# Moving a quarter of the modulation projection from a feed-forward stage into a delta-rule recurrence, with an idle product ahead of each solve

## The chip, the core and the metric

The kernel runs as one program on one core of a Trainium2 chip. The metric is device time in microseconds from start to end of the program. All data is float32.
## What is computed

Two blocks of two layers each work on 512 tokens of width 1024. The first block has attention mixers and gated feed-forward layers (1024 to 2816 to 1024). The second block has a mixer with a bidirectional gated delta rule and pooling, an expert-choice feed-forward, a short-convolution mixer and a second expert-choice feed-forward. Each norm of the second block is modulated by vectors that depend on the conditioning alone:

```python
for i in range(DEPTH):                                        # second block, DEPTH = 2
    sh1_l, sc1_l, g1_l, sh2_l, sc2_l, g2_l = jnp.split(jax.nn.silu(c) @ ada_w[i] + ada_b[i], 6, axis=-1)
    hl = modulate(rms_norm(xl, norm_mix[i]), sh1_l, sc1_l)    # then the mixer, scaled by g1_l
    ...
    hl2 = modulate(rms_norm(xl, norm_ffn[i]), sh2_l, sc2_l)
    xl = xl + g2_l[:, None] * expert_choice_ffn(hl2, router[i], w_gate[i], w_up[i], w_down[i])

# gated delta rule, chunks of 64 tokens, 4 heads, forwards and backwards; context (256 tokens) first, then the 512 tokens
t_mat = eye + where(strict, kk * decay, 0) * beta[..., None]
u = solve(t_mat, v * beta[..., None]);  wk = solve(t_mat, k * (beta * exp(gam))[..., None])
w = u_c - einsum(wk_c, s);  s = cd_c * s + einsum(kd_c, w)
```

`ada_w` is (2, 1024, 6144). Of layer 1, the last three of the six vectors (sh2, sc2, g2) are first read in the last quarter of the program, by the norm before the second expert layer and by that layer.

## The kernel before

**The modulation.** Class `Modulation` computes both layers' 6144 outputs in 12 groups of 1024 outputs, each group in 4 parts, 48 parts in all. A part reads one panel of 1 MB (`fetch`, two buffers in `arena`). The stationary operand is `cond`, two columns (the conditioning of the tokens and of the context), and the moving operand is weights, 256 columns. One group's outputs are laid over four strips of PSUM partitions (0, 32, 64, 96), so that the four products of a round stand in four column strips of the array. A part is 8 products (L1129): 2 of the 8 tiles of the contraction times 4 strips. After four parts `keep` copies 2 by 256 values from each strip, and after all twelve groups `turn` transposes everything (96 small transposes, L1146) and `add` adds it to the biases.

**Where it runs.** All of it runs in the first gated feed-forward of the first block. PE works there through 20 quads of seven blocks each (`GatedUnits.quad_products`, L467: 4 products per block, 8 records). `ada_between` puts one part after the second, fourth and sixth block of a quad: parts 2 to 47 stand in quads 0 to 15, and `turn` stands in quad 17. `mod.part` waits for its panel; SyncE issues the panels in a row with the feed-forward's own weights.

**The recurrence.** `even_mixer` runs `DeltaChain` in 6 steps (`STEPS`; steps 0 and 1 are the context, `LAT_FROM` = 2). A step handles 128 tokens in each of two directions d. The order of each engine is written out by hand:

- `keys` (L2167), `level_z` (L2180) and `level_update` (L2194) build the inverse of the triangular matrix in 6 levels (`LEVELS`), each product being 64 by 64. After each, VectorE masks or subtracts (`level_mask` L2439, `level_x` L2443, `level_y` L2447), and PE waits for that.
- `solve` (L2251, L2258) uses the finished inverse `Y`. It waits for `y_solved`, `k_done` and `v_done` of both directions, from step 2 on also for `qk_done`, which VectorE's `within_rows` (L2455) gives.
- In the next step `use_state` (L2274) waits until ScalarE has copied the result of the solve (`keep_solved`, L2368). Then `new_state` (L2284) and `outputs` (L2296, L2300) update the state.
- `turn_keys` (L2205) and `turn_values` (L2218) transpose keys and values.

`stay_busy(k, pe, bank, n, cols)` (L114) issues n products whose result nobody reads. The recurrence has one of 256 columns ahead of `use_state` in steps 1 to 5, and three after `turn_keys` in steps 1 and 2. SyncE loads the output projection's four panels (`out.fetch`, L3912) before step 2 into four buffers (three in `h`, one in `gate_rows`), and for each step from 2 on the gate rows (`fetch_gates`, L2133) and the growth rows (`fetch_growth`, L2144), in this order, each behind its own waits.

## Time and profile before

| | us |
|---|---|
| median of 3 runs | 2789.36 (2783.68 to 2789.53) |
| the profiled execution, its own time | 2787.13 |
| span of its trace | 2785.3 |
| first gated feed-forward with the modulation, 415 to 712 | 297 |
| recurrence, six steps, 1726 to 1941 | 215 |

A row of the timeline gives the start of a run of like records, the time they cover, the engine, the line, the tiles and shapes, the number of records, and in brackets how long the engine sat idle before and what it waited for. [...] The time around the span of the profiled execution is 1.8 us.

### The profile page before, as it was taken

What the parts mean: (1) busy time and instruction counts of PE and PEld (TensorE: products, weight loads), DVE (VectorE), ACT (ScalarE), POOL (GpSimd) and SP (SyncE); (2) the same over time, 40 slices, a digit from 0 to 9 for tenths busy, and PEclk for the clock granted to TensorE, in tenths of its full rate; (3) what the DMA queues carried; (4) which work ended last, traced back from release to release, by engine and by line L of the source; (5) the groups of instructions that cost most, each with busy time, mean ns of one, the idle gap of its engine ahead of it and who ended that gap; (6) DMA issues with size and microseconds to landing.
All of it is one profiled execution on the core that took longest, in us unless ns stands there. A gap on an engine that the chain in (4) does not pass through costs nothing. (4 is left out here: it accounts for less than half of the span.)

```text
span 2785.3 us, 36571 instructions
## 1 busy us (share of the span) xinstructions
PE 2710.5 (97%) x15316; PEld 1801.6 (65%) x15316; DVE 1162.6 (42%) x2250; ACT 525.9 (19%) x1164; POOL 626.2 (22%) x450
## 2 busy tenths in 40 slices
PE   8999999999999999999999999899989999998998
PEld 5564477777886445888888755888733338873333
DVE  2325534444413233544433485656232235652223
ACT  1344410000001133110000232433110120011011
POOL 3250004333341010344443410010010003531000
PEclk9999999999999999999999999999999999999999
DMA  8211026775222211222221402100399972239994
GB/s 268 103 46 46 31 91 248 266 266 183 84 98 88 91 72 46 91 84 83 72 83 42 190 17 78 39 21 7 154 367 421 420 301 76 92 123 365 421 421 198
DMA packets 70045, 431.23 MB, mean 155 GB/s; under 512 B 8203, under 2 KB 9018, under 8 KB 25721
## 3 DMA queue, kind: packets, MB, share of 16 engines
q1 hardware_dynamic: 65080, 412.56, 38.7%
q0 software_dynamic: 4800, 16.33, 1.7%
q8 instruction: 122, 2.00, 0.3%
q14 instruction: 43, 0.34, 0.0%
HBM read 422.41 MB, written 13.79 MB: 157 GB/s over the span
## 5 line engine op out<-in xcount | busy, mean ns | idle before, releaser
L467 PE MATMUL bank<-h,weight_ring 128*128 128x256 f32 x960 | 230.3, 383 | 1.1 <-DVE arena L391 1.0
L467 PEld LDWEIGHTS bank<-h,weight_ring 128*128 128x128 f32 x960 | 179.8, 190 | 38.4 <-issue 13.7
L622 PE MATMUL bank<-arena,weight_ring 128*128 128x256 f32 x704 | 155.0, 379 | 0.0
L467 PE MATMUL bank<-h,arena 128*128 128x256 f32 x640 | 151.2, 379 | 0.0
L622 PEld LDWEIGHTS bank<-arena,weight_ring 128*128 128x128 f32 x704 | 133.8, 190 | 18.4 <-issue 0.4
L3038 PE MATMUL bank<-weight_slots,tokens_T 128*64 128x512 f32 x592 | 141.7, 593 | 2.1 <-issue 2.1
L467 PEld LDWEIGHTS bank<-h,arena 128*128 128x128 f32 x640 | 121.7, 190 | 16.4
L427 POOL TENSOR_TENSOR arena<-weight_ring 128x512 f32<-128x512 f32 x40 | 52.8, 1320 | 352.5 <-PE bank L467 309.5
L3581 PE MATMUL bank<-h,weight_slots 128*128 128x256 f32 (+1 forms) x384 | 128.9, 491 | 0.8 <-ACT h L2705 0.8
L3077 PE MATMUL bank<-logits_or_select,h 128*128 128x512 f32 x256 | 118.2, 600 | 1.7 <-DVE h L3207 1.7
L622 PE MATMUL bank<-arena 128*128 128x256 f32 x528 | 117.1, 380 | 0.0
L325 PE MATMUL bank<-arena,weight_ring 128*128 128x256 f32 (+1 forms) x384 | 116.4, 454 | 0.0
L1440 PE MATMUL bank<-weight_ring,h 128*128 128x512 f32 x256 | 113.3, 597 | 0.0
L622 PEld LDWEIGHTS bank<-arena 128*128 128x128 f32 x528 | 100.3, 190 | 14.3 <-DVE x L664 0.4
L1440 PE MATMUL bank<-h,weight_ring 128*128 128x512 f32 (+2 forms) x304 | 107.4, 507 | 0.6 <-DVE h L273 0.6
L3581 PEld LDWEIGHTS bank<-h,weight_slots 128*128 128x128 f32 x384 | 71.5, 190 | 56.1 <-issue 46.5
L3038 PE MATMUL bank<-weight_ring,tokens_T 128*64 128x512 f32 x432 | 105.0, 592 | 0.0
L3038 PEld LDWEIGHTS bank<-weight_slots,tokens_T 128*64 128x64 f32 x592 | 49.6, 137 | 81.1 <-issue 79.2
L897 DVE COPY arena<-bank 128x512 f32<-128x512 f32 x96 | 61.9, 685 | 91.8 <-PE bank L906 62.5
L3198 DVE TENSOR_TENSOR hidden<-bank,hidden 128x512 f32<-128x512 f32 x16 | 11.1, 691 | 211.5 <-PE bank L3038 211.5
L325 PEld LDWEIGHTS bank<-arena,weight_ring 128*128 128x128 f32 x384 | 71.2, 190 | 39.0 <-issue 32.6
L1440 PEld LDWEIGHTS bank<-weight_ring,h 128*128 128x128 f32 x256 | 47.6, 190 | 62.9 <-issue 59.5
(607 smaller groups left out, 4746.0 us busy)
## 6 DMA issues: line engine op xcount, KB each, us to landing
arena<-in_ada_w SPq DMA_DIRECT2D x48, 1024.0 KB, 6.9
weight_ring<-in_gu SPq DMA_DIRECT2D x44, 1024.0 KB, 4.9
weight_slots<-in_w_up SPq DMA_DIRECT2D x42, 1024.0 KB, 26.0
weight_slots<-in_w_down SPq DMA_DIRECT2D x34, 1024.0 KB, 21.5
weight_slots<-in_w_gate SPq DMA_DIRECT2D x32, 1024.0 KB, 23.2
weight_ring<-in_w_gate SPq DMA_DIRECT2D x32, 1024.0 KB, 23.2
weight_ring<-in_w_down SPq DMA_DIRECT2D x30, 1024.0 KB, 24.1
weight_ring<-in_down SPq DMA_DIRECT2D x32, 704.0 KB, 4.4
```

Of the source, the lines that this page charges most:

```text
L325: m = pe.matmul(bank, self.slots[i].buf[:, at * P:(at + 1) * P], self.src(c)[:, lo:hi], start=(c == 0), stop=(c == self.kt - 1))
L427: g.tensor_tensor(s1, self.block(q, 1, 0), self.block(q, 1, 1), ALU.add).then_inc(self.summed.sem, 1)
L467: m = pe.matmul(self.bank(q, i), weights[:, c * P:(c + 1) * P], tokens[:, c, :], start=(c == 0), stop=(c == 3))
L622: m = pe.matmul(self.bank(u, name), lhs[:, j * P:(j + 1) * P], rhs, start=(j == 0), stop=(j == self.DEPTH - 1))
L897: v.tensor_copy(self.prob_T[:, c % 2, s, :], self.k.bank[:, 4 + s, :]).then_inc(self.copied.sem, 1)
L1440: m = pe.matmul(out, lhs, rhs, start=(c == 0), stop=(c == last - 1))
L3038: m = pe.matmul(self.k.bank[e * CAP:(e + 1) * CAP, 3 + j, :], self.tok_T[:, r % 2, 4 * half + c, e * CAP:(e + 1) * CAP], slot.buf[:, c * D ...
L3077: m = pe.matmul(self.k.bank[:, 2 if n % 2 == 0 else 5, :], self.y[:, self.place(r), c * P:(c + 1) * P], self.sel[:, self.place(r), :], sta ...
L3198: v.tensor_tensor(self.hid[:, :], self.k.bank[:, 4, :], self.hid[:, :], ALU.mult).then_inc(self.product.sem, 1)
L3581: m = pe.matmul(self.bank(n)[:, 0:hi - lo], slot.buf[:, at:at + P], self.h[:, c, lo:hi], start=(c == 0), stop=(c == KT - 1))
```

## The change

`Modulation` keeps 36 parts in 9 groups (layer 0, and the first half of layer 1). A new class `LateModulation` computes the other 12 parts, 3 groups, in the recurrence: one part ahead of `use_state` in steps 1 and 2 and two in steps 3 to 5; two parts after `turn_keys` in steps 1 and 2. The weights are laid out so that a late part covers all 8 tiles of the contraction and a quarter of the columns: 32 products of 64 columns each, in four strips. The idle products at these places go. `solve` now waits for keys, values and queries first, then issues one idle product of 256 columns, and then waits for `y_solved`. Four buffers hold the late panels, the same four that `out.fetch` fills later; each panel of either kind is issued when the part that read the buffer is done.

```diff
 class Modulation:
-    STRIPS, STRIP, WIDTH, GROUPS, PARTS = 4, 32, 256, 12, 4
+    STRIPS, STRIP, WIDTH, GROUPS, PARTS, LAYER = 4, 32, 256, 9, 4, 24
...
+class LateModulation:
+    FIRST, GROUPS, DEPTH = 9, 3, 4
...
+    def fetch(self, sp, n, weights):
+        if n >= self.DEPTH:
+            after(sp, self.done, n - self.DEPTH)
+        sp.dma_start(self.panels[self.place(n)], weights[n]).then_inc(self.landed[self.place(n)].sem, 16)
+
+    def part(self, pe, n):
+        g, i = divmod(n, Modulation.PARTS)
...
+        w = Modulation.WIDTH // Modulation.PARTS
+        for t in range(KT):
+            for s in range(Modulation.STRIPS):
+                at, panel = s * STRIP, (t * Modulation.STRIPS + s) * w
+                m = pe.matmul(self.bank(g)[at:at + 2, i * w:(i + 1) * w], self.cond[:, t, :], self.panels[self.place(n)][:, panel:panel + w],
+                              start=(t == 0), stop=(t == KT - 1))
+        m.then_inc(self.done.sem, 1)
+
+    def keep(self, v, g):
+        after(v, self.done, (g + 1) * Modulation.PARTS - 1)
+        v.tensor_copy(self.rows[:, g, :], self.bank(g)).then_inc(self.kept.sem, 1)
...
+    def turn(self, pe):
...
+        for g in range(self.GROUPS):
+            for j in range(2):
+                m = pe.matmul(out[:, g, :, j], self.rows[:, g, j * P:(j + 1) * P], self.k.ident[:, 0:P:STRIP], start=True, stop=True)
...
     def solve(self, pe, j):
         for d in range(2):
-            after(pe, self.y_solved[d], LEVELS * (j + 1) - 1)
             after(pe, self.k_done[d], j)
             after(pe, self.v_done[d], j)
             if j >= LAT_FROM:
                 after(pe, self.qk_done[d], j - LAT_FROM)
+        stay_busy(self.k, pe, 6, 1, HALF)
+        for d in range(2):
+            after(pe, self.y_solved[d], LEVELS * (j + 1) - 1)
...
+        PARTS_AT = {(1, 0): (0,), (1, 1): (1, 2), (2, 0): (3,), (2, 1): (4, 5), (3, 0): (6, 7), (4, 0): (8, 9), (5, 0): (10, 11)}
...
+                late.fetch(sp, 0, a["ada_late"])
...
-                for i in range(4):
-                    out.fetch(sp, i, a["ev2_out"])
+                late.fetch(sp, 1, a["ada_late"])
                 c.store_growth(sp)
                 for j in range(LAT_FROM, STEPS):
                     c.fetch_gates(sp, j)
+                    for n in {2: (2,), 3: (3, 4, 5), 4: (8,), 5: (11,)}[j]:
+                        late.fetch(sp, n, a["ada_late"])
                     c.fetch_growth(sp, j)
+                    for n in {3: (6, 7), 4: (9, 10)}.get(j, ()):
+                        late.fetch(sp, n, a["ada_late"])
+                for i in range(4):
+                    after(sp, late.done, late.parts - late.DEPTH + (i + 1) % 4)
+                    out.fetch(sp, i, a["ev2_out"])
...
                 for j in range(STEPS):
                     if j:
-                        stay_busy(k, pe, 3, 1, HALF)
+                        late_parts(j, 0)
                         c.use_state(pe, j - 1, 0)
...
-                    if 0 < j <= LAT_FROM:
-                        stay_busy(k, pe, 3, 3, HALF)
+                    if j:
+                        late_parts(j, 1)
...
                         c.level_update(pe, j, 1, n)
+                        if n == 2 and j == LAST:
+                            late.turn(pe)
...
                         c.level_y(v, j, 0, n)
+                        if n == 1 and j in (2, LAST):
+                            late.keep(v, 0 if j == 2 else 2)
+                        if n == 3 and j == LAST:
+                            late.add(v)
...
                         c.level_y(v, j, 1, n)
+                        if n == 1 and j == 3:
+                            late.keep(v, 1)
```

How PE's order changes at the end of step 2 and the start of step 3 (`vectors` holds `cond`, `h` and `gate_rows` the panels, `constants` the idle product's operands; here one product is one). Before:

```order
L2167 MATMUL bank<-weight_slots 64x64 [waits delta_masked0]
L2167 MATMUL bank<-weight_slots 64x64 x7
L2251 MATMUL bank<-delta_work,weight_slots 128x64 [waits delta_y_solved,delta_k_done,delta_qk_done,delta_v_done]
L2251 MATMUL bank<-delta_work,weight_slots 128x64 x15
L2258 MATMUL bank<-weight_slots,delta_work 64x128 x16
L114 MATMUL bank<-constants 128x256
L2274 MATMUL bank<-state,weight_slots 64x128 [waits delta_advanced,delta_scaled,delta_uw_kept]
```

The same place on PE in the changed kernel:

```order
L2225 MATMUL bank<-weight_slots 64x64 x7
L114 MATMUL bank<-constants 128x256 [waits delta_k_done,delta_v_done,delta_qk_done]
L2311 MATMUL bank<-delta_work,weight_slots 128x64 [waits delta_y_solved]
L2311 MATMUL bank<-delta_work,weight_slots 128x64 x15
L2318 MATMUL bank<-weight_slots,delta_work 64x128 x16
L1197 MATMUL bank<-h,vectors 2x64 [waits ada1_landed]
L1197 MATMUL bank<-h,vectors 2x64 x31
L1197 MATMUL bank<-h,vectors 2x64 [waits t5_in0]
L1197 MATMUL bank<-h,vectors 2x64 x31
L2334 MATMUL bank<-state,weight_slots 64x128 [waits delta_advanced,delta_scaled,delta_uw_kept]
```

The idle product has moved from behind the solve to ahead of it, and 64 products of two late parts stand where it stood. On the same engine, in step 2 of the changed kernel after `turn_keys` (L2263):

```order
L2263 MATMUL bank<-constants,weight_slots 128x128 x3
L1197 MATMUL bank<-gate_rows,vectors 2x64 [waits t5_in1]
L1197 MATMUL bank<-gate_rows,vectors 2x64 x31
L1197 MATMUL bank<-h,vectors 2x64 [waits ada0_landed]
L1197 MATMUL bank<-h,vectors 2x64 x31
L2252 MATMUL bank<-delta_work 64x64 [waits delta_masked0]
```

Two parts stand there in place of three idle products. SyncE's queue in the middle of the changed recurrence:

```order
L1186 DMA gate_rows<-in_ada_late 128x2048 [waits ada_part]
L2202 DMA weight_slots<-growth_scratch 128x512 [waits delta_q_done] x2
L1186 DMA h<-in_ada_late 128x2048 [waits ada_part] x2
L2191 DMA gate_rows<-gate_scratch 64x512 [waits delta_a]
L2191 DMA gate_rows<-gate_scratch 64x512 x3
L1186 DMA h<-in_ada_late 128x2048 [waits ada_part]
```

Late panels stand between the gate rows and the growth rows, each behind the part that frees its buffer.

## Rows read from the trace of the kernel before

**Rows 1.** The page: busy us, share of the span, instructions of each engine

```profile
PE 2710.5 (97%) x15316; PEld 1801.6 (65%) x15316; DVE 1162.6 (42%) x2250; ACT 525.9 (19%) x1164; POOL 626.2 (22%) x450
```

**Rows 2.** Stretches: length, busy PE, PEld, DVE, ACT, POOL, PEclk, DMA share, GB/s

```profile
415.00:712.00 297.00, 295.31 (x1963) 221.47 (x1962) 132.93 (x255) 23.43 (x58) 106.49 (x80) 1.00 0.64 232
1789.60:1827.20 37.60, 32.99 (x698) 29.55 (x696) 24.12 (x51) 14.18 (x47) 5.93 (x4) 0.93 0.10 31
1863.60:1902.20 38.60, 36.70 (x740) 33.94 (x738) 22.61 (x51) 15.37 (x51) 5.52 (x4) 0.93 0.06 16
```

**Rows 3.** Timeline of PE, first gated feed-forward

```profile
640.63 1.04 PE L1129 MATMUL bank<-arena,vectors 128*2 128x256 f32 x16
...
645.26 1.04 PE L1129 MATMUL bank<-arena,vectors 128*2 128x256 f32 x16
...
676.38 1.89 PE L467 MATMUL bank<-h,weight_ring 128*128 128x256 f32 x8
...
679.83 1.89 PE L467 MATMUL bank<-arena,weight_ring 128*128 128x256 f32 x8
...
697.19 1.65 PE L1146 MATMUL bank<-constants,arena 2*128 2x2 f32 x96
698.77 1.99 PE L467 MATMUL bank<-h,weight_ring 128*128 128x256 f32 x8
```

**Rows 4.** Timeline of PE, recurrence, where late parts go in step 1

```profile
1757.62 0.70 PE L114 MATMUL bank<-constants 128*128 128x256 f32 x2
1758.53 1.09 PE L2274 MATMUL bank<-state,weight_slots 128*64 128x128 f32 x16 [0.21 <-ACT weight_slots L2368]
...
1767.58 1.46 PE L114 MATMUL bank<-constants 128*128 128x256 f32 x6
1769.37 1.15 PE L2194 MATMUL bank<-delta_work 64*64 64x64 f32 x32 [0.33 <-DVE delta_work L2439]
```

**Rows 5.** Timeline of PE, the solves of steps 0, 2, 3 and 4

```profile
1752.89 0.69 PE L2167 MATMUL bank<-kv_ctx 128*64 128x64 f32 x16
1753.79 2.00 PE L2251 MATMUL bank<-delta_work,weight_slots 64*128 64x64 f32 x32 [0.21 <-issue]
...
1820.78 2.91 PE L2251 MATMUL bank<-delta_work,weight_slots 64*128 64x64 f32 x32 [0.64 <-DVE delta_work L2447]
...
1828.37 1.13 PE L2274 MATMUL bank<-state,weight_slots 128*64 128x128 f32 x16
...
1859.81 2.00 PE L2251 MATMUL bank<-delta_work,weight_slots 64*128 64x64 f32 x32 [0.64 <-DVE delta_work L2447]
...
1864.54 1.09 PE L2274 MATMUL bank<-state,weight_slots 128*64 128x128 f32 x16 [0.21 <-ACT weight_slots L2368]
...
1895.83 2.87 PE L2251 MATMUL bank<-delta_work,weight_slots 64*128 64x64 f32 x32 [0.73 <-DVE delta_work L2447]
...
1903.38 1.17 PE L2274 MATMUL bank<-state,weight_slots 128*64 128x128 f32 x16
```

**Rows 6.** Timeline of PE, one update of two directions in step 2

```profile
1805.17 2.08 PE L2194 MATMUL bank<-delta_work 64*64 64x64 f32 x64
```

**Rows 7.** Timeline of DVE, the mask before that update; the last subtraction of step 2

```profile
1804.69 0.89 DVE L2439 TENSOR_TENSOR delta_work<-bank,delta_masks 128x256 f32<-128x256 f32 x2
...
1819.90 0.41 DVE L2447 TENSOR_TENSOR delta_work<-delta_work,bank 128x256 f32<-128x256 f32 x1
```

**Rows 8.** Groups of PE records by form: busy us, mean ns, idle before

```profile
L2981 PE MATMUL bank<-constants,h 128*128 128x16 f32 x8 | 1.1, 265 | 0.0
```

**Rows 9.** Timeline of PE, in a stretch with one-column weights

```profile
2497.55 0.59 PE L2885 MATMUL bank<-h,constants 128*1 128x512 f32 x1 [1.16 <-ACT h L2833]
```

**Rows 10.** That stretch, columns as in Rows 2

```profile
2494.00:2501.00 7.00, 5.84 (x31) 2.45 (x30) 1.67 (x5) 2.19 (x5) 0.00 (x0) 1.00 0.75 270
```

**Rows 11.** Timeline of SyncE's queue: an issue in the recurrence

```profile
1798.31 1.74 SPq L2144 DMA_DIRECT2D weight_slots<-growth_scratch  x2
```

**Rows 12.** DMA issues: engine, count, KB each, median us to landing

```profile
h<-in_ev_out SPq DMA_DIRECT2D x3, 1024.0 KB, 8.0
```

More of the change, by code:

```diff
@@ L1108, in fetch @@
             after(sp, self.done, n - 2)
-        sp.dma_start(self.panels[:, n % 2, :], weights[2 * n // self.parts][n % (self.parts // 2)]).then_inc(self.landed[n % 2].sem, 16)
+        sp.dma_start(self.panels[:, n % 2, :], weights[n // self.LAYER][n % self.LAYER]).then_inc(self.landed[n % 2].sem, 16)
     def sigmoids(self, a):
@@ L1537, in _ @@
                     mod.fetch(sp, n, ada)
-                gated0.slots[FT - 1].fetch(sp, a["gu0"][FT - 1])
+                for t in range(17, FT):
+                    gated0.slots[t].fetch(sp, a["gu0"][t])
                 down0.fetch(sp, 0, a["down0"])
@@ L3993, in even_mixer @@
         coming = Ahead(k, 15, 12 * ROUNDS)
+        late = LateModulation(k, vec["cond"].rearrange("p (t c) -> p t c", c=2), out_bufs,
+                              dm["run_fwd"].rearrange("p (g n) -> p g n", n=Modulation.WIDTH), vec["ada_b1"][:, 24:48])
+        PARTS_AT = {(1, 0): (0,), (1, 1): (1, 2), (2, 0): (3,), (2, 1): (4, 5), (3, 0): (6, 7), (4, 0): (8, 9), (5, 0): (10, 11)}
         LAST = STEPS - 1
@@ L4088, in _, with late_parts @@
                 pe.wait_ge(units.done.sem, units.done.at(len(units.order) - 1))
+                def late_parts(j, place):
+                    for n in PARTS_AT.get((j, place), ()):
+                        late.part(pe, n)
                 c.keys(pe, 0, 0)
@@ L4790, in more_layout @@
     }
+    late = i["ada_w_2"][1].reshape(KT, P, 6, Modulation.STRIPS, Modulation.PARTS, -1)[:, :, 6 - LateModulation.GROUPS:]
+    out["ada_late"] = late.transpose(2, 4, 1, 0, 3, 5).reshape(-1, P, SLOT)
     for layer in range(2):
```

24 lines of the change are left out of this document (23 added, 1 removed).

## The prediction, made before the changed kernel ran

> **What bounds the kernel now.** I read the page first: PE is busy for 97% of the span and the next engine for 65%, so a microsecond of PE work that goes anywhere is nearly a microsecond of time, unless another engine takes over there [rows 1]. Then the stretches. From 415 to 712 us, where all 48 modulation parts run, PE is busy 295.31 of 297 us while VectorE has 133 and GpSimd 106 [rows 2]: PE alone sets the pace. In the recurrence PE is busy most of the time too, yet it waits for others at a few fixed places, and the granted clock is not full: 0.93 in two stretches of some 38 us [rows 2]. The timeline shows where. The solves of steps 2, 3 and 4 each come after 0.64 to 0.73 us of idle PE. From the start of the solve to the next `use_state` it takes 4.73 us in step 3 (1859.81 to 1864.54), but 7.59 in step 2 (1820.78 to 1828.37) and 7.55 in step 4 (1895.83 to 1903.38) [rows 5]. [...]
>
> **The parts that leave the feed-forward.** Two parts start 4.63 us apart with two blocks between them (640.63 to 645.26); two blocks without a part take 3.45 us (676.38 to 679.83) [rows 3]. So a part costs 1.17 us there, and twelve of them 14.0 us. `turn` has 96 records from 697.19 to 698.77, 0.0165 us each; it loses 24, which is 0.4 us [rows 3]. Nothing takes over: the blocks from 676.38 to 697 already run without parts at the same 1.73 us per block. Sum: 14.4 us gained, all on the path.
>
> **What a late part costs.** A part's 16 records of 256 columns take 1.04 us, while the same records in full width take 3.45/16 = 0.216 us each, 3.45 in all [rows 3]. So four run at a time, one in each strip. A late part has 64 records of 64 columns. If only the columns counted, it would need 16 rounds of 0.216/4 = 0.054, 0.86 us. If the rate at which PE takes short records counts, the nearest row is `turn`, also four at a time: 64 times 0.0165 is 1.06 us [rows 3]. The recurrence's own 64 by 64 records, two at a time, take at most 2.08/64 = 0.0325 us [rows 6], which would make 2.1 us. I take 1.06, since `turn` shares the four-way overlap, and add 0.15 for the change of shape behind a group of parts (an estimate from the 0.97 plus two slightly stretched blocks around a part in the feed-forward); 0.86 and 2.1 are the ends. [...]
>
> **What of it is hidden.** Ahead of `use_state` PE has 0.91 us (1757.62 to 1758.53) until ScalarE's copy arrives, filled by an idle product that goes [rows 4]. One part (1.21) overshoots by 0.30, two (2.27) by 1.36: 2 times 0.30 plus 3 times 1.36 is 4.7 us. After `turn_keys` it has 1.79 us (1767.58 to 1769.37) until VectorE's mask, filled by three idle products [rows 4]; two parts overshoot by 0.48, in steps 1 and 2, 1.0 us. All overshoot counts in full: what follows on PE waits for nothing but what `use_state` itself starts. Together 5.7 us.
>
> **Small additions in the recurrence.** PE's update at 1805.17 starts 0.06 us after the first of the two masks ends (1804.69 plus half of the 0.89) [rows 6, 7], so VectorE has no slack at that place. Each `keep` of 128 by 256 there costs about one such operation, 0.42 us, in steps 2 and 5; the one in step 3 stands ahead of `turn_values` and costs perhaps 0.2. Sum 1.0. The late `turn` is 12 records with 128-column weights; the nearest row has 8 in 1.1 us [rows 8], so 1.6 us, in a dense stretch of PE, and `add` behind it 0.15. Sum 1.8.
>
> **The solve.** Now the last subtraction ends at 1819.90 + 0.41 = 1820.31, and the solve starts at 1820.78, 0.47 later [rows 5, 7], where an update follows its mask by 0.06. The difference is the other waits, which PE works off one by one behind `y_solved`. The change puts them ahead. An idle product then stands between: two records of 0.216 us, and about 0.1 until another shape may start. In steps 2 to 4 it can start when `within_rows` is done, about when the last subtraction starts, and it ends around 1820.6: 0.15 us gained each. In steps 0 and 1 there is less room: `keys` starts at 1752.89 and the solve at 1753.79 [rows 5]; the product adds about 0.35 each. In step 5 it comes after two idle products that stay, and adds 0.3. Sum 0.55 us lost; bounds -1 and +2.5.
>
> **The clock.** If the idle product keeps the clock up, 7.59 - 4.73 and 7.55 - 4.73, 5.7 us, come back. It replaces idle time of PE by full-width work just ahead of the place where the clock fell. The two-column parts replace full-width idle products at other places, so I looked for narrow products elsewhere: from 2494 to 2501 us PE works with one-column weights and idles 1.16 us, and the granted clock stays 1.00 [rows 9, 10]. I take both falls as gone.
>
> **Transfers.** SyncE now issues late panels between gate and growth rows. A 1 MB panel lands in about 8 us [rows 12]. Panels 6 and 7 stand behind the growth rows issued at 1798.31 [rows 11] and are needed when step 3 begins after 1827, with some 20 us to spare; the others have as much or more. The output panels come last, the first when parts 8 and 9 are done (about 1866), the rest after parts 10 and 11 (about 1906); the output projection starts near 1946. Nothing is late, cost 0; without that cover a panel would cost up to its 8 us.
>
> **Sum** against the profiled execution's own 2787.13: -14.0 - 0.4 - 5.7 (clock) + 5.7 (parts) + 1.0 + 1.8 + 0.55 = -11.1, so 2776.0 us. The median of the runs shown is 2789.36, 2.2 higher, which may be one more fall; I don't add it, since the changed kernel should have none.
>
> **Rivals.**
> - The idle product does not hold the clock. For: the gap before the last update of a step (0.5 us) stays. Against: the larger gap is filled. The 5.7 us stay lost: 2781.7.
> - Late parts cost 0.0325 us per record, as 64 by 64 records do. For: the length is the same. Against: those are two at a time. 12 times 1.02 is 12.2 us: 2788.2. [...]
> - The two-column parts let the clock fall, because they fill so few columns of the array. Pairs stand alone at five places. Five falls of 2.85 us above the forecast: 2790.3, no change. Rows 9 and 10 speak against it.
> - Slower: the four strips do not overlap at 64 columns, since each product's two records must follow each other in one strip. Then a part takes 64 times 0.054 = 3.5 us, 12 times 2.4 = 29 us more: 2805. It decides from a part of 2.7 us on, where the sum passes 2795. Both the `turn` and the part at 256 columns, which has the same two records per product, speak against it.
> - The change doesn't do what it says: panels arrive late and PE waits at the parts, at most 8 us each; the order above leaves no place for it. About 2790.
> - More is hidden than I think: a part of 0.86 us saves another 0.2 at each, 2.4 us, and the solves start earlier: 2772.
>
> **Chances.** Forecast (2773 to 2779.5) 0.55; better (below 2773) 0.12; clock not held 0.13; slow records 0.09, two thirds of them in the milder form; clock falls at parts 0.06; slower 0.03; panels late 0.02. The range that holds 8 in 10 runs from 2770 to 2785: it takes in the forecast, most of the better case, the unheld clock and the milder slow records. A measurement of this kernel tells a change of about 0.2%, 5.6 us, from none; that puts the bounds at 2783.8 and 2795. Faster has 0.55 + 0.12 + 0.13 + 0.06 = 0.86, same 0.10, slower 0.04.
>
> **What would show it.** In the first feed-forward no part between 620 and 675 us and the stage 14 us shorter. In the recurrence parts of 1.0 to 1.1 us each; `use_state` waiting for nothing in steps 3 to 5; an idle product within the gap ahead of the solve, which follows the subtraction by less than 0.4 us; a granted clock of 1.00 throughout; the recurrence 3 us longer than now, or 9 longer if the clock fell as often. I am wrong if the records of a late part start more than 0.02 us apart on average, or if a clock of 0.5 shows near a pair of parts.

## The result: 0.2% slower, and where the time went

The changed kernel takes 2789.8 us (median of 20 runs, 2784.7 to 2795.6), the kernel before 2784.7 us (median of 20 runs beside them, 2780.6 to 2791.2). The ratio is 1.002 with a 95% interval of 1.0013 to 1.0026: slower by 5 us, where 2776.0 was forecast with a range from 2770 to 2785. The profiled execution of the changed kernel took 2792.8 us, with a span of 2791.0.

The page hardly tells the two apart. PE is busy for 97% of the span as in [rows 1]:

```profile
PE 2711.4 (97%) x15870; PEld 1814.3 (65%) x15870; DVE 1158.1 (41%) x2242; ACT 525.9 (19%) x1164; POOL 627.8 (22%) x450
```

The gain in the feed-forward is there. The `turn` that started at 697.19 [rows 3] starts at 683.04 and is shorter, and up to there PE is busy as fully as it was [rows 2]. The timeline of PE at that place, and the stretch 415 to 698 (length, busy PE, PEld, DVE, ACT, POOL, mean granted clock with 1.00 as full, DMA share, GB/s):

```profile
683.04 1.28 PE L1147 MATMUL bank<-constants,arena 2*128 2x2 f32 x72
684.25 2.00 PE L467 MATMUL bank<-h,weight_ring 128*128 128x256 f32 x8
...
415.00:698.00 283.00, 282.81 (x1758) 220.39 (x1757) 131.54 (x249) 23.43 (x58) 107.32 (x80) 1.00 0.55 199
```

The recurrence starts 14.5 us earlier (its first `keys` at 1712.1 instead of 1726.6). But from there to the first product of the output projection it takes 241.8 us instead of 220.1, 21.7 more, where I had 3 more. (Two later profiles of the kernel before take 214.2 and 215.3 us there, so the loss is larger still.) Four stretches of the changed kernel, from solve to solve (steps 1 to 4), same columns:

```profile
1740.80:1779.40 38.60, 33.20 (x852) 30.31 (x851) 21.36 (x50) 14.18 (x47) 0.00 (x0) 0.91 0.27 98
1779.40:1821.90 42.50, 35.29 (x884) 31.92 (x883) 24.04 (x52) 14.18 (x47) 5.93 (x4) 0.92 0.32 102
1821.90:1866.10 44.20, 39.18 (x869) 36.37 (x868) 22.80 (x53) 15.36 (x51) 5.52 (x4) 0.92 0.35 97
1866.10:1902.90 36.80, 35.83 (x867) 33.25 (x866) 22.55 (x52) 15.37 (x51) 5.53 (x4) 1.00 0.14 46
```

Step 4 is as it should be: PE busy for 35.83 of 36.80 us, clock 1.00. Steps 1 to 3 are 5 to 7 us too long, PE idles in them, and the granted clock is 0.91 to 0.92. What ends the idle time is in the waits of PE from 1708 to 1945 us (line, releaser: us in total, times, longest us). The view of the kernel before has no such rows among the levels:

```profile
PE bank L2238 <- issue: 5.2, 2, 3.4
...
PE bank L2252 <- issue: 3.7, 2, 1.9
...
PE bank L2292 <- issue: 2.3, 1, 2.3
```

These are 11.2 us in five gaps, released by "issue": by nothing that the profile shows. And they lie inside groups of like products, where no wait can stand. The timeline of PE at the first gap:

```profile
1756.73 1.15 PE L2252 MATMUL bank<-delta_work 64*64 64x64 f32 x32
1757.71 0.87 PE L2238 MATMUL bank<-delta_work 64*64 64x64 f32 x24
1761.98 0.69 PE L2238 MATMUL bank<-delta_work 64*64 64x64 f32 x8 [3.40 <-issue]
1762.46 3.62 PE L2252 MATMUL bank<-delta_work 64*64 64x64 f32 x64
```

Of 32 records of one `level_z`, 24 run, PE stands still for 3.40 us, and then come the other 8. The next update takes 3.62 us instead of the 2.08 of [rows 6]: the granted clock is 0.50 from 1761.1 to 1767.8. So it is behind all five gaps, with 0.50 also from 1802.0, 1812.2, 1853.2 and 1860.0 on, for 3.4 us each time.

What was in flight? SyncE's issues just ahead, in the timeline of its queue, are the gate rows of step 3 and three late panels:

```profile
1750.92 3.07 SPq L2191 DMA_DIRECT2D gate_rows<-gate_scratch  x4
1754.04 0.59 SPq L1186 DMA_DIRECT2D h<-in_ada_late  x1
1754.66 0.43 SPq L1186 DMA_DIRECT2D gate_rows<-in_ada_late  x1
1755.97 0.33 SPq L1186 DMA_DIRECT2D h<-in_ada_late  x1
```

The DMA view has a queue 8 named "instruction", whose packets are 16 KB (126 packets with 2.06 MB on the page). Their number goes with PE's records: 126 for the 31740 of this kernel, 122 for the 30632 of the kernel before, 120 for the 30224 of e12_neither below, one for every 251 or 252. From 1752.4 to 1759.6 us it has none, though PE works through the first 6 of these 7 us, until it stands still at 1758.6 (queue, kind: packets, MB, share of the 16 engines):

```profile
q1 hardware_dynamic: 506, 1.95, 79.7%
q14 instruction: 1, 0.01, 0.4%
```

From 1759.6 to 1761.0 it has one, beside DMA engines busy for 99% with data:

```profile
q1 hardware_dynamic: 74, 0.57, 99.0%
q8 instruction: 1, 0.02, 4.2%
```

Read packet by packet from the same trace, that fetch runs from 1759.70 to 1760.63, and PE goes on 1.35 us after its end. The five gaps in one table (PE's records are products and weight loads together):

```
gap us   PE goes on   fetch          from its end   PE records since the fetch before began
3.40     1761.98      1759.70-60.63  1.35           476
1.87     1802.33      1800.00-00.94  1.38           502
1.82     1810.46      1807.87-09.01  1.45           272
1.85     1851.70      1849.16-50.10  1.60           531
2.25     1859.56      1857.04-58.11  1.45           288
```

My reading, theory A: TensorE's instructions come over the same DMA engines as the data (the view counts queues 1 and 8 as shares of the same 16), the fetch waits behind the loads that are already issued, and PE runs out of instructions. Theory B: the late parts do it by themselves, since a part is 128 records in 1.07 us (products and loads) and so uses up the instructions in hand. Theory C: the clock is the loss, and the narrow parts pull it down.

### The profile page after: what moved, and what is told of

Read it like the earlier page. It is cut to its first block and busy times, and to the rows that moved or that the text cites. A ratio compares the mean times of both kernels' runs of the same rounds, so it can differ in the third digit from the quotient of the medians.

```text
span 2791.0 us, 37669 instructions
## 1 busy us (share of the span) xinstructions
PE 2711.4 (97%) x15870; PEld 1814.3 (65%) x15870; DVE 1158.1 (41%) x2242; ACT 525.9 (19%) x1164; POOL 627.8 (22%) x450
## 3 DMA queue, kind: packets, MB, share of 16 engines
q8 instruction: 126, 2.06, 0.3%
## 5 line engine op out<-in xcount | busy, mean ns | idle before, releaser
L467 PEld LDWEIGHTS bank<-h,arena 128*128 128x128 f32 x640 | 121.8, 190 | 16.3
L1497 PEld LDWEIGHTS bank<-h,weight_ring 128*128 128x128 f32 (+1 forms) x304 | 56.9, 192 | 49.2 <-issue 45.5
```

Of the source, the lines that this page charges most:

```text
L467: m = pe.matmul(self.bank(q, i), weights[:, c * P:(c + 1) * P], tokens[:, c, :], start=(c == 0), stop=(c == 3))
L1497: m = pe.matmul(out, lhs, rhs, start=(c == 0), stop=(c == last - 1))
```

## The experiments

All times are medians; each group of experiments was measured beside runs of the kernel before on the same chip, whose medians are 2783.1 to 2784.0 us. "Stretch" is the time from the first `keys` to the first output product in the profiled execution. The gaps counted are those of PE released by "issue". e1, e2 and e12 leave out loads or parts, so a part of their modulation is wrong or missing. One of the six runs of e12_neither took 6171 us; the ratio leaves it out, and its cause is not known.

```
run                    us       ratio to before, 95%     stretch   "issue" gaps over 0.7 us
before (profile above) 2784.7   -                        220.1     none
changed                2789.8   1.002  [1.0013,1.0026]   241.8     5, 11.2 us
e1_few_loads           2776.2   0.9972 [0.9961,0.9983]   224.3     1, 2.6
e2_loads_alone         2779.9   0.999  [0.9981,0.9999]   230.5     5, 10.9
e3_spread_loads        2773.5   0.9964 [0.9950,0.9978]   222.0     none
e9_spread_again        2773.4   0.9966 [0.9953,0.9978]   222.2     none
e18_spread_new_solve   2772.7   0.9959 [0.9945,0.9972]   223.0     2, 1.9
e6_spread_old_solve    2771.5   0.9961 [0.9948,0.9975]   221.9     none
e17_spread_old_solve   2772.1   0.9958 [0.9944,0.9972]   220.9     none
e8_trios_after_gates   2774.6   0.9971 [0.9962,0.9981]   223.5     2, 2.6
e14_quarters           2787.3   1.0014 [1.0005,1.0023]   235.5     6, 11.7
e4_old_solve           2793.6   1.0035 [1.0022,1.0048]   242.3     5, 12.0
e12_neither            2767.1   0.9939 [0.9927,0.9952]   214.7     none
e5_before_new_solve    2783.0   1.0    [0.9991,1.0009]   216.0     none
e7_burst_sizes         2782.6   (one run)                215.1     none
e10_bursts_in_levels   2791.1   (one run)                225.3     3, 4.2
e15_before_look        2781.4   0.999  [0.9980,1.0000]   214.2     none
e16_before_look_2      2784.6   1.0001 [0.9990,1.0011]   215.3     none
```

### Take most of the loads away, keep every instruction of PE

(A part waits only for the first landing in its place, so that none waits for a load that is gone.)

```diff
-                    for n in {2: (2,), 3: (3, 4, 5), 4: (8,), 5: (11,)}[j]:
+                    for n in {2: (2,), 3: (3,)}.get(j, ()):
                         late.fetch(sp, n, a["ada_late"])
                     c.fetch_growth(sp, j)
-                    for n in {3: (6, 7), 4: (9, 10)}.get(j, ()):
-                        late.fetch(sp, n, a["ada_late"])
```

> The changed kernel with eight of its twelve late panel loads left out: panels 0 to 3 are loaded where they were, panels 4 to 11 are not, and parts 4 to 11 read what lies in their places (so those parts of the modulation are wrong; the instructions of TensorE are the same). Theory A (the 1 MB loads, issued two or three in a row beside the gate loads, keep the instruction fetches of TensorE waiting, and it runs dry in the middle of a group of products): the five stalls of 1.8 to 3.4 us, 11.2 us in all, are gone, and with them the clock falls that stand right behind them; time 2789.8 - 11.2 - 2 or 3 of clock = 2776 to 2778. Theory B (the parts themselves, 128 instructions in a microsecond, empty the instruction buffer, whatever is loaded): all five stalls stay, time 2789 to 2791. Theory C (the clock falls are the loss and come from the two-column parts, the stalls are a sign of something else): falls stay at the same places, time above 2785.

Measured 2776.2 us. Four of the five gaps are gone, all those where no panel is loaded now, though PE runs the same instructions. One stays, and its place is telling: it is where panel 3 still follows the four gate loads, 1 MB behind four times 128 KB. The timeline of PE:

```profile
1760.20 0.69 PE L2238 MATMUL bank<-delta_work 64*64 64x64 f32 x8 [2.61 <-issue]
```

This goes against theory B and against theory C: the parts are all there, and the clock stays at 1.00 in steps 2 to 5 (1763.7 to 1902.0). It goes to 0.50 once, at this one gap (1760.3 to 1763.6). The expectation had this gap gone too.

### Keep the loads, take the parts away

```diff
-                        late_parts(j, 0)
+                        stay_busy(k, pe, 3, 1, HALF)
...
-                    if j:
-                        late_parts(j, 1)
+                    if 0 < j <= LAT_FROM:
+                        stay_busy(k, pe, 3, 3, HALF)
```

(The `keep`s, the late `turn` and `add` go too, and a load waits for the landing of the one before it in its place.)

> The changed kernel without its twelve late parts, their keeps, turn and addition (that third of the modulation is left out), with the idle products of the kernel before in their places, but with all twelve 1 MB loads issued as in the changed kernel, each after the one that filled its place before has landed. Theory A: without the parts TensorE takes 128 instructions fewer for each, so it runs dry later or less, but the loads still delay the fetches: two to five stalls of 0.5 to 3 us at the same places; time 2789.8 - 8 (parts, keeps, turn) - 2 to 6 = 2776 to 2780. Theory B: no stall at all, and time 2768 to 2772.

Measured 2779.9 us. The timeline of PE, the rows behind a gap of over 0.7 us:

```profile
1798.13 1.43 PE L2252 MATMUL bank<-delta_work 64*64 64x64 f32 x21 [2.06 <-issue]
...
1837.05 1.14 PE L2238 MATMUL bank<-delta_work 64*64 64x64 f32 x30 [0.93 <-issue]
...
1845.46 1.80 PE L2292 MATMUL bank<-weight_slots 128*64 128x64 f32 x30 [3.94 <-issue]
...
1881.59 0.39 PE L2238 MATMUL bank<-delta_work 64*64 64x64 f32 x6 [1.93 <-issue]
...
1887.80 0.45 PE L2292 MATMUL bank<-weight_slots 128*64 128x64 f32 x7 [2.07 <-issue]
```

The loads alone bring 10.9 us of gaps, as much in sum as in the changed kernel. But the last two, 4.0 us, come from the four output panels, which this kernel issues among the levels of step 4. The late panels alone bring 6.9 us in three gaps, against 11.2 us in five with the parts, and the three panels behind the gate rows in step 1 bring none over 0.7 us. So the loads are enough to make gaps, and theory B, the parts by themselves, is out; but the parts use up instructions and make the gaps longer, as the expectation had it. e12_neither, with neither loads nor parts, has no such gap:

> The changed kernel without the late third of the modulation: no late loads, parts, keeps, turn or addition (that third is left out), the idle products and the loading of the output panels as in the kernel before; the first nine groups and the new solve stay. It gives the term of the feed-forward stage by itself: 2784 - 14.4 = 2769 to 2771. The distance from it to e3_spread_loads (2773.4) is the price of the late parts and all that goes with them: 2.5 to 4.5 us, where the prediction had 8.5.

Measured 2767.1 us, 2 us under what was expected, stretch 214.7. Its distance to e3_spread_loads below is 6.4 us, where the expectation had 2.5 to 4.5. Loads alone add 12.8 us to it by the medians and 15.8 by the stretches. That is more than the gaps: the granted clock is 0.50 at two of them, from 1797.9 and from 1845.7 on, and once in step 0, from 1716.0 on, for 3.4 us each. In the changed kernel the excess over e12_neither is 27.1 us: 11.2 of gaps, 6.5 of parts (below), and the other 9 are what is left. The clock accounts for them by an estimate from the stretches of steps 1 to 3 above: 0.09 of 38.6, 0.08 of 42.5 and 0.08 of 44.2 us is 10.4 us of lost clock. So a gap costs nearly twice its length where the clock goes down at it.

### Keep everything, spread the loads

```diff
+                def late_alone(sp, j, first, last):
+                    after(sp, c.gates_in[j % 2], j // 2)
+                    after(sp, late.done, first - 2)
+                    for n in range(first, last):
+                        if n > first:
+                            after(sp, late.landed[late.place(n - 1)], (n - 1) // late.DEPTH)
+                        late.fetch(sp, n, a["ada_late"])
...
-                    for n in {2: (2,), 3: (3, 4, 5), 4: (8,), 5: (11,)}[j]:
-                        late.fetch(sp, n, a["ada_late"])
+                    if j == 2:
+                        late.fetch(sp, 2, a["ada_late"])
+                    else:
+                        late_alone(sp, j, *{3: (4, 7), 4: (7, 10), 5: (10, 12)}[j])
                     c.fetch_growth(sp, j)
-                    for n in {3: (6, 7), 4: (9, 10)}.get(j, ()):
-                        late.fetch(sp, n, a["ada_late"])
+                    if j == 2:
+                        after(sp, late.landed[late.place(2)], 0)
+                        late.fetch(sp, 3, a["ada_late"])
```

> The changed kernel, complete, with the late panel loads spread: panel 3 once panel 2 has landed, panels 4 to 6 one at a time after part 2 and after the gate loads of step 3 have landed, panels 7 to 9 in the same way after part 5 and the gate loads of step 4, panels 10 and 11 after part 8 and those of step 5; never two in flight together. Theory A: one panel delays a fetch by under 3 us, which the 256 or more instructions in hand cover; no stall over 0.5 us; time 2775 to 2779, faster than the kernel before by 0.2 to 0.35%. Theory B: the five stalls stay where the parts are; 2788 to 2791.

The "256 or more instructions in hand" go by the trace of the changed kernel, where a fetch comes for every 252 records of PE; how many PE has in hand at a fetch no run counts. The 3 us can be estimated from a stretch there with full DMA engines, 421 GB/s from 1759.6 to 1761.0: 1 MB takes 2.5 us at that rate.

Measured 2773.5 us, ratio 0.9964: faster than the kernel before by 10 us and than the changed one by 16. Only the order and the waits of SyncE differ; all twelve panels are loaded. The timeline of its queue in step 2, where the changed kernel issued growth, two panels, gates and a panel within 6 us:

```profile
1786.46 1.74 SPq L2202 DMA_DIRECT2D weight_slots<-growth_scratch  x2
1788.30 2.38 SPq L2191 DMA_DIRECT2D gate_rows<-gate_scratch  x4
1794.55 0.34 SPq L1186 DMA_DIRECT2D h<-in_ada_late  x1
1800.20 0.34 SPq L1186 DMA_DIRECT2D gate_rows<-in_ada_late  x1
1805.06 0.33 SPq L1186 DMA_DIRECT2D h<-in_ada_late  x1
```

A panel has landed before the next is issued, some 5 us later, and no wait of PE for a panel shows in the recurrence. The long gaps are gone; "issue" among the levels has this much left, a little over the 0.5 us that was expected at most:

```profile
PE bank L2252 <- issue: 0.6, 1, 0.6
```

And steps 1 to 4 are now this long, at a full clock (columns as above; solve to solve):

```profile
1740.10:1773.80 33.70, 30.96 (x852) 27.92 (x851) 21.34 (x49) 14.18 (x47) 0.00 (x0) 1.00 0.32 112
1773.80:1809.20 35.40, 31.87 (x885) 28.78 (x884) 24.06 (x52) 14.18 (x47) 5.93 (x4) 1.00 0.36 122
1809.20:1846.10 36.90, 35.93 (x869) 33.30 (x868) 22.77 (x53) 15.37 (x51) 5.53 (x4) 1.00 0.09 32
1846.10:1882.90 36.80, 35.82 (x867) 33.23 (x866) 22.55 (x52) 15.37 (x51) 5.52 (x4) 1.00 0.32 103
```

The same kernel was measured twice more, 2773.4 and 2772.7 us:

> The kernel of e3_spread_loads once more, beside the other three: 2772 to 2776, faster than before by 0.25 to 0.45%, no stall of TensorE over 0.7 us in the recurrence.

> The kernel of e3_spread_loads again, for the comparison with e17_spread_old_solve: 2772 to 2776.

The gaps are not gone in every execution. The profile of e9 has one of 0.5 us, that of e18 has two of nearly 1 us, with one panel at a time in flight. The timeline of PE in e18:

```profile
1765.37 0.68 PE L2252 MATMUL bank<-delta_work 64*64 64x64 f32 x16 [0.89 <-issue]
...
1798.21 0.38 PE L2252 MATMUL bank<-delta_work 64*64 64x64 f32 x5 [0.97 <-issue]
```

### Length of a burst, size of a transfer, and where a burst falls

e8_trios_after_gates takes only the line `after(sp, late.landed[...])` and the `if` above it out of `late_alone`.

> The kernel of e3_spread_loads with panels 4 to 6, 7 to 9 and 10 to 11 issued back to back again, but still only once the gate loads of the step have landed. If the length of the burst is what counts: stalls of 1 to 4 us after the two bursts of three and none or a small one after that of two, 2776 to 2780. If it is the mixture with the gate loads: no stall, 2773 to 2775.

Measured 2774.6 us, with two gaps of 1.3 us. So most of what spreading gives, 15 of 16 us, is there as soon as the panels keep clear of the gate and growth rows in flight. What issuing the panels one by one adds, 2.6 us of gaps against 0 to 1.9 and 1 to 2 us by the medians, is within the noise of the runs.

e14_quarters loads each panel of the changed kernel as four transfers (and a part waits for all four):

```diff
-        sp.dma_start(self.panels[self.place(n)], weights[n]).then_inc(self.landed[self.place(n)].sem, 16)
+        for q in range(4):
+            cols = slice(q * 512, (q + 1) * 512)
+            sp.dma_start(self.panels[self.place(n)][:, cols], weights[n][:, cols]).then_inc(self.landed[self.place(n)].sem, 16)
```

> The changed kernel with each late panel loaded as four transfers of a quarter of its columns (2 KB a row instead of 8 KB), issued in the same places. If the fetch waits for the amount of data ahead of it: the stalls stay, 2788 to 2793. If it waits for one long transfer and gets its turn between short ones: the stalls shrink to under 1 us each, 2776 to 2780.

Measured 2787.3 us with 11.7 us of gaps: shorter transfers don't shorten them. The stretch is 6.3 us shorter than that of the changed kernel all the same, since the clock goes down at one of the six gaps only. The length of one transfer is out as the cause. That the amount of data ahead of the fetch is what counts isn't shown by this, and it can't be all: in e1_few_loads 1.5 MB, a panel behind four gate loads, bring a gap of 2.6 us, and in e8_trios_after_gates 3 MB without gate loads bring 1.3. What in the gate loads makes it worse stays open.

e7_burst_sizes and e10_bursts_in_levels put bursts of one to four panels into the kernel before, where no late part is. The diff is that of e7; in e10 `burst` waits with `after(sp, c.y_solved[0], LEVELS * j + 1)`:

```diff
...
-                for i in range(4):
-                    out.fetch(sp, i, a["ev2_out"])
+                def burst(j, n):
+                    after(sp, c.uw, j)
+                    for i in range(n):
+                        out.fetch(sp, i, j, a["ev2_out"])
...
                     c.fetch_gates(sp, j)
+                    if j > LAT_FROM:
+                        burst(j - 2, j - 2)
                     c.fetch_growth(sp, j)
+                burst(4, 4)
```

> The kernel before with its four output panels loaded later and again and again: one 1 MB load after the solve of step 1, two after that of step 2, three after that of step 3, four after that of step 4 (the last ones are the ones used); no late parts. Nothing else is in flight there. Theory A (a fetch of instructions queues behind the data that is already in the rings, 1 MB being some 2.6 us at 400 GB/s): one panel no stall, two none or under 1 us, three 1 to 3 us, four 3 to 6 us, each in the step's next group of products. Rival (only loads beside the gate loads' small packets, or only beside the parts, starve the fetch): no stall after any of the four bursts, time as before.

The 400 GB/s are what the traces show while the DMA engines are full: 421 GB/s in the changed kernel from 1759.6 to 1761.0 us, and in the kernel before from 2100 to 2200, so a megabyte takes some 2.5 us. The four gate loads issued from 1750.92 on in the changed kernel are 256 packets of 2 KB; a panel's packets have 8 KB. That a fetch queues behind the data ahead of it is the theory on trial here, and its stalls are my estimates.

Behind the solves not one gap, even with four panels in flight, and 2782.6 us as before. Theory A as I had put it failed here: a burst is not enough. The fetch was late all the same: behind the burst of four (issued from 1897.4 to 1899.5) it starts at 1902.39, 345 records after the fetch before, where in e16_before_look_2, with no burst, 262 records lie between the same two. What differs, by this reading, is how fast PE takes instructions. Behind a solve it waits for state updates and takes 128-row products: from the start of each of the four bursts it takes 8.9 to 9.5 us for 256 records. Among the levels the fastest 256 records take 3.8 us. So the second run, the same bursts among the levels:

> The kernel of e7_burst_sizes with the same bursts of one, two, three and four 1 MB loads (steps 1, 2, 3, 4), each now released when the first direction has solved its second level of that step, in the middle of the stretch in which TensorE takes 256 instructions in under 4 us; nothing else is in flight. In e7_burst_sizes four loads right behind a solve cost nothing. If a fetch waits for the data ahead of it and the instructions in hand last longer behind a solve than among the levels: no stall for one load, up to 1 us for two, 1 to 3 us for three, 3 to 5 us for four. If loads alone, without the gate loads beside them, never starve the fetch: no stall.

Measured 2791.1 us. From the start of each of its four bursts PE takes 256 records in 4.9 to 5.0 us. The timeline of PE, the rows behind gaps:

```profile
1850.67 1.67 PE L2194 MATMUL bank<-delta_work 64*64 64x64 f32 x50 [1.11 <-issue]
...
1856.07 1.20 PE L2194 MATMUL bank<-delta_work 64*64 64x64 f32 x34 [1.10 <-issue]
...
1895.48 0.45 PE L2194 MATMUL bank<-delta_work 64*64 64x64 f32 x9 [1.97 <-issue]
```

The expectation says that nothing else is in flight, but that is not so. SyncE's timeline has the bursts right behind the growth and gate rows (four gate loads ahead of the bursts of two and three, two growth loads ahead of that of four):

```profile
1841.10 2.87 SPq L2133 DMA_DIRECT2D gate_rows<-gate_scratch  x4
1844.07 1.48 SPq L3914 DMA_DIRECT2D h<-in_ev_out  x3
1878.24 1.56 SPq L2144 DMA_DIRECT2D weight_slots<-growth_scratch  x2
1880.00 2.91 SPq L3914 DMA_DIRECT2D h<-in_ev_out  x3
```

Against e7_burst_sizes the time from solve to solve is 0.1 us longer with one panel (32.05 to 31.97), 0.4 with two (35.45 to 35.03), 2.7 with three (38.79 to 36.06), and 2.7 with four (38.72 to 36.03), where another 3.9 follow (40.67 to 36.80) since the granted clock is 0.50 from 1897.6 on, behind the last gap, for 10.2 us. So the kernel before, with no late part and no edit to the solve, shows gaps like those of the changed one from a burst of three panels on, the three behind gate loads. Since the neighbours of the bursts changed along with their place, these two runs, one execution each, don't tell place and mixture apart. Between three and four my sizes were too regular: the fourth panel added nothing.

One more reading holds all of this together. In the eight traces with gaps over 0.7 us (changed, e1, e2, e4, e8, e10, e14, e18) there are 29 of them. In all 29 PE goes on 1.26 to 1.60 us after the end of a packet of queue 8. In 16 of the 17 gaps that are the first behind a burst, 404 to 543 records of PE lie between the start of the fetch before and the gap. In the other it is 357, and in the two of e18, which has no burst, 335 and 400; there the fetch before was late itself. Undisturbed, a new fetch starts for every 252 on average (e12_neither, 180 to 386 among those of the recurrence). At the first gap of each of the three bursts of the changed kernel the fetch starts 3.6 to 4.4 us after PE's 256th record. That loads make a fetch wait for some 4 us is what these runs add.

### The solve and the clock

```diff
     def solve(self, pe, j):
         for d in range(2):
-            after(pe, self.y_solved[d], LEVELS * (j + 1) - 1)
             after(pe, self.k_done[d], j)
             after(pe, self.v_done[d], j)
             if j >= LAT_FROM:
                 after(pe, self.qk_done[d], j - LAT_FROM)
+        stay_busy(self.k, pe, 6, 1, HALF)
+        for d in range(2):
+            after(pe, self.y_solved[d], LEVELS * (j + 1) - 1)
```

e5 puts this edit into the kernel before; e6 and e17 take it out of e3's kernel; e4 takes it out of the changed kernel.

> The kernel before with only the edit to the solve: an idle product of 256 columns after the waits on the kept keys and values and ahead of the wait on the last level. By the prediction's terms: +0.35 us at the two context steps each, -0.1 at steps 3 and 5, and the clock held at the solves of steps 2 and 4 (5.7 us): 2784.7 - 5 = about 2779.5. If the falls of the clock at the solves are not cured by it: 2784.5 to 2786.

> The kernel of e3_spread_loads with the solve of the kernel before (no idle product, the wait on the last level first). If the new solve pays what the prediction put on it (clock held at the solves of steps 2 and 4, 5.7 us, against 0.35 us at each of two steps): slower than e3_spread_loads by about 4 to 5 us, 2778. If it only pays where the clock would have fallen, and with the parts in the steps the clock no longer falls there: within 1.5 us of e3_spread_loads, 2773 to 2775.

> The changed kernel with the solve of the kernel before. By the prediction's clock term it loses 4 to 5 us against the changed kernel (2794). By e5_before_new_solve and e6_spread_old_solve, in which the new solve was worth nothing that shows, it is within 2 us of it: 2788 to 2791, with the five stalls unchanged.

Measured: 2783.0 (ratio 1.0), 2771.5 beside 2773.4 for e9 on the same chip, and 2793.6, which is the number of the prediction's clock term, though its interval overlaps that of the changed kernel (and its stretch, 242.3, is like 241.8). In the first two the edit is worth nothing that shows; the third leaves up to 4 us open. The timeline of e4 has what the edit was meant to cure, at the solve of step 2:

```profile
1816.16 3.00 PE L2309 MATMUL bank<-delta_work,weight_slots 64*128 64x64 f32 x32 [0.64 <-DVE delta_work L2505]
```

How often does this happen in the kernel before? It was profiled twice more, and the pair with spread loads measured again:

> The kernel before, unchanged, profiled again. If the two clock falls at the solves of steps 2 and 4 that the prediction counted (5.7 us) belong to every execution: they are there again, and the stretch from the first keys to the first output product is about 220 us. If they come only in some executions: fewer or none, 215 to 218 us.

> The kernel before once more, with the same two expectations: 220 us and both falls, or 215 to 218 us and fewer.

> The kernel of e6_spread_old_solve again, beside the new solve on the same chip. If the new solve holds the clock in every execution: 4 to 5 us slower than e18_spread_new_solve. If what it saves comes only in some executions and is partly paid back at the context steps: within 1.5 us of it.

The falls at the solves of steps 2 and 4 are in neither new profile. The timeline of PE in e15_before_look at the solves of steps 2 and 3, and the stretch behind the first:

```profile
1819.03 2.00 PE L2251 MATMUL bank<-delta_work,weight_slots 64*128 64x64 f32 x32 [0.64 <-DVE delta_work L2447]
...
1855.16 2.00 PE L2251 MATMUL bank<-delta_work,weight_slots 64*128 64x64 f32 x32 [0.64 <-DVE delta_work L2447]
...
1821.00:1857.00 36.00, 34.18 (x739) 31.62 (x738) 22.64 (x51) 15.36 (x51) 5.51 (x4) 1.00 0.10 32
```

The same gap of 0.64 us as in [rows 5], but the solve takes 2.00 us, not 2.91, and the clock is 1.00; in the profile of [rows 5] it is 0.50 from 1821.7 to 1828.4. Six profiles here have the old solve and no loads among the levels that bring gaps over 0.7 us (before, e15, e16, e7, and with spread loads e6 and e17). One of the six, the one I had, shows the falls. With e4 and e10, which have gaps, it is two of eight; of the ten profiles with the new solve none has a fall that starts at a solve. So the new solve may well hold the clock, but where loads bring no gaps there is seldom a fall to hold off. And e17_spread_old_solve took 2772.1 us beside the 2772.7 of e18: no difference.

## Why the prediction was wrong, step by step

- **Transfers, "Nothing is late, cost 0"**: this is the step that failed, and it alone turns the sign. Its count was right, no part waits for a panel. But it asked only whether a load comes in time, not what it holds up on the way. Nine loads of 1 MB, issued among the levels within 6 us of others or of the gate rows, held up the instruction fetches: 11.2 us of gaps and about 9 us more, mostly the clock at them. By the medians, what spreading the loads gives back: 2789.8 - 2773.5 = 16.3 us.
- **Feed-forward, -14.4**: right. 14.15 us at the `turn`, and 0.37 in it (1.65 to 1.28 us).
- **A late part**: the form of the sum was right. The timeline of PE in the changed kernel, a single in step 1 and a pair in step 3, both ahead of `use_state`:

```profile
1744.67 1.07 PE L1197 MATMUL bank<-gate_rows,vectors 128*2 128x64 f32 x64
1745.67 1.09 PE L2334 MATMUL bank<-state,weight_slots 128*64 128x128 f32 x16
...
1825.72 1.97 PE L1197 MATMUL bank<-h,vectors 128*2 128x64 f32 x128
1827.62 1.09 PE L2334 MATMUL bank<-state,weight_slots 128*64 128x128 f32 x16
```

  From start to next start a single takes 1.00 us and a pair 1.90, 0.0148 us a record, where I had 0.0165 and 0.15 on top: 2.27 for a pair. The row of `turn` was the right one to go by, and both rivals with slower records are out. The chances also name a milder form of slow records, beside the one of 0.0325 us. No run shows a term for it: the records of a late part start 14.8 ns apart.
- **Parts, keeps and late turn, +8.5 together**: 6.5. From e12_neither to e3_spread_loads the times from solve to solve grow by 1.36, 0.39, 1.00, 1.00 and 2.78 us (the whole stretch by 7.3, and by 7.5 and 8.4 in e9 and e18, whose steps 1 and 2 are up to 1.5 us longer; e18 has its two "issue" gaps there, and the 1.36 of e3's step 1 hold the one of 0.6). The pairs ahead of `use_state` cost 1.00, not 1.36, and in step 2 the parts and the `keep` hide better than I thought, at 0.39 for 1.2. The late `turn` was 1.43 us to the next start, for 1.6.
- **The solve, +0.55**: the size is about right; by the stretches of e16 and e5 it is 0.7 (215.3 to 216.0). From the kernel before (e16) to e5 the solves come 0.35 us later in step 1, 0.04 earlier in each of steps 2 to 4, where I had 0.15, and 0.17 later in step 5. The idle product takes 0.60 us from its start to that of the solve (1821.30 to 1821.90 in the changed kernel), where the prediction counted two records of 0.216 and about 0.1 for the next shape, 0.53. It stands right behind `keys`, and the solve starts 0.42 us after the last subtraction (1821.48), where it had been 0.47; that the other waits made up the difference of the 0.47 to the 0.06 of an update was my estimate.
- **The clock, -5.7**: mis-sized by nearly all of it. Without bursts among the levels it was 0 to 2 us against the median, since the falls were those of one execution out of six. With them, in the changed kernel itself, e4_old_solve leaves up to 4 us open. I counted both in full, as a certain gain, with one execution to go by. In the rival "clock not held" the 5.7 us were lost by falls that stay; in truth there was mostly nothing to hold. That the two-column parts don't pull the clock down was right: e3 and e8 have them, e12 hasn't, and all three have the clock at 1.00 in steps 1 to 5. So the sign that I had named for being wrong, a clock of 0.5 near a pair of parts, did show in the changed kernel, but it belongs to the gaps.
- **The sum, as it would be without the failed step**: from the median of before, 2784.7 - 14.5 + 6.5 + 0.5 = 2777.2 with the clock at 0; e3 measured 2772.7 to 2773.5 in three runs. About 1 to 2 us of the rest is that the runs of before behind e3 were 2783 to 2784; the other 2 to 3 us I can't place. e12_neither has the same excess: 2767.1 where 2784.0 - 14.5 + 0.5 gives 2770. That e3 lies within the forecast's 2773 to 2779.5 is luck in part: the 5.7 us of the clock weren't there, and a base that was 2.4 us too high, parts that were 2.0 too dear and the rest that I can't place made up for them.
- Of the chances: by the bounds of the prediction, 2783.8 to 2795, the result counts as "same", which had 0.10; beside 20 runs of the kernel before it is slower, which had 0.04. None of the rivals was this one; two had a number near the result (the clock falling at pairs, 2790.3, and panels late, about 2790), by other mechanisms and so by luck. The panels did cost time, but not as the rival "panels late" said, by PE waiting at the parts.

## What to carry to other kernels

When a change adds loads, ask not only whether they land in time but what else uses the DMA engines meanwhile, and the instruction fetch does (here a packet of 16 KB for every 252 records of PE). In stretches of many short instructions issue a large transfer only once the small ones ahead of it have landed (one panel behind four gate loads cost a gap of 2.6 us in e1), and rather one at a time; put bursts where the engine takes its instructions slowly, as behind a solve here (256 records in 8.9 to 9.5 us, against 3.8 at the fastest among the levels). Even so, one of the three profiles of the spread kernel kept two gaps of nearly 1 us. A gap released by "issue" in the middle of a group of like instructions is the sign to look for, with the packets of the instruction queue beside it. And a loss that one profiled execution shows, the clock above all, is counted in full only when a second execution shows it too.

## What was unexpected of the hardware

- TensorE ran dry for 0.8 to 4.2 us at a time (at the first gap of the changed kernel the DMA engines were 80 to 99% busy with data); it went on 1.26 to 1.60 us after its instruction packet had come (29 of 29 gaps).
- A panel of 1 MB behind four small gate loads held PE up for 2.6 us (e1), three panels in a row without them for 1.3 (e8), and four in a row behind a solve not at all (e7).
- Cutting 1 MB transfers into quarters changed the gaps from 11.2 to 11.7 us: nothing.
- At such a gap the granted clock went to 0.50 in all five cases of the changed kernel, though in only one of six in e14_quarters (from 1801.7 on). The gap of 0.64 us ahead of the solves, in contrast, was followed by a fall in one profile of six, or two of eight with those that have other gaps.
- 64-column records with two-column weights, in four strips, start 14.8 ns apart on average.
